# Three fused blocks on one core: an attention unit's order, the first loads, which rows of the third block stand in which stage, and a decay factor kept in three places

## The reference

```python
# first block: short conv, conformer conv (31 taps), differential attention
y_sc   = (sc_b * causal_dwconv(sc_c * sc_x, sc_conv)) @ sc_out
y      = causal_dwconv(a * sigmoid(gate), conf_conv) + conf_conv_b   # 31 taps
a      = softmax(q1 k1) - lam * softmax(q2 k2)                       # 4 heads x 4 query blocks
# third block: z, r are silu(...) rows, gates are sigmoid(...) rows, xs/bm/cm pass a 4-tap conv
o_a = rms_norm(gla(...), gla_norm_w) * silu(r)
o_b = ssd_scan forward + backward + d_skip * x;  o_b = rms_norm(o_b * silu(z))
merged = sigmoid(gate_a) * (o_a @ w_pa) + sigmoid(gate_b) * (o_b @ w_pb)
```

## Time and profile before

| | us |
|---|---|
| median of 3 runs (lowest, highest) | 3657.41 (3651.36, 3658.62) |
| the profiled execution | 3653.29 |
| its span | 3651.3 |

### The profile page before, as it was taken

The page is one execution under the profiler, slowest core; times in us unless marked ns, Lnnn a source line. Parts: engine busy times, 40 slices in busy tenths (PEclk is TensorE's granted clock), DMA queues, the critical chain, the costliest instruction groups (busy, mean ns, idle before and its releaser), DMA issues. The chain is left out here.

```text
span 3651.3 us, 44458 instructions
## 1 busy us (share of the span) xinstructions
PE 3279.2 (90%) x17672; PEld 2613.6 (72%) x17672; DVE 2141.3 (59%) x2499; ACT 1254.9 (34%) x1906; POOL 1360.4 (37%) x625
## 2 busy tenths in 40 slices
PE   7989998999989898988999988989989757789997
PEld 5767876888856677966888867767876545668885
DVE  6366965889855476344746574867974676531112
ACT  4223343323243332233323342333433354332222
POOL 3423434444422234434444432326631222334442
PEclk9989999999989999999999989989999879899998
DMA  3213354465333245344344232423334445422322
GB/s 115 87 58 113 118 159 152 144 224 180 127 113 99 75 133 157 123 163 155 121 145 155 69 111 89 153 83 118 105 111 126 156 141 162 133 81 81 110 84 66
DMA packets 237261, 447.05 MB, mean 122 GB/s; under 512 B 59792, under 2 KB 119888, under 8 KB 230272
## 3 DMA queue, kind: packets, MB, share of 16 engines
q1 hardware_dynamic: 229984, 433.73, 36.5%
q10 hardware_dynamic: 7072, 10.49, 0.8%
HBM read 394.78 MB, written 49.37 MB: 122 GB/s over the span
## 5 line engine op out<-in xcount | busy, mean ns | idle before, releaser
L356 POOL TENSOR_TENSOR third_feed_lo<-third_feed_raw,third_feed_hi 128x1024 fp32r<-128x1024 f32 (+3 forms) x191 | 445.4, 2335 | 836.2 <-ACT third_feed_hi L349 819.8
L356 POOL TENSOR_TENSOR second_feed_lo<-second_feed_raw,second_feed_hi 128x1024 fp32r<-128x1024 f32 (+3 forms) x182 | 405.4, 2229 | 667.0 <-ACT second_feed_hi L349 637.8
L356 POOL TENSOR_TENSOR first_feed_lo<-first_feed_raw,first_feed_hi 128x1024 fp32r<-128x1024 f32 (+4 forms) x182 | 394.9, 2174 | 601.0 <-ACT first_feed_hi L349 591.2
L273 PE MATMUL shared_ps<-third_h_hi,third_feed_hi 128*128 128x512 f32 (+1 forms) x776 | 327.4, 422 | 66.9 <-ACT lgate_rows_bend L875 14.5
L274 PE MATMUL shared_ps<-third_h_lo,third_feed_hi 128*128 128x512 f32 (+1 forms) x776 | 314.2, 405 | 0.0
L275 PE MATMUL shared_ps<-third_h_hi,third_feed_lo 128*128 128x512 f32 (+1 forms) x776 | 313.9, 405 | 0.0
L349 ACT ACTIVATE third_feed_hi<-third_feed_raw 128x1024 fp32r<-128x1024 f32 (+3 forms) x191 | 190.8, 1001 | 278.7 <-PE ffn_low L275 79.1
L349 ACT ACTIVATE second_feed_hi<-second_feed_raw 128x1024 fp32r<-128x1024 f32 (+3 forms) x182 | 173.9, 956 | 211.0 <-PE ffn_low L275 70.8
L273 PEld LDWEIGHTS shared_ps<-third_h_hi,third_feed_hi 128*128 128x128 f32 (+1 forms) x776 | 153.2, 197 | 116.2 <-issue 77.7
L273 PE MATMUL mixer_acc<-first_h_hi,first_feed_hi 128*128 128x512 f32 x544 | 224.4, 413 | 11.3 <-DVE first_h_lo L428 7.4
L349 ACT ACTIVATE first_feed_hi<-first_feed_raw 128x1024 fp32r<-128x1024 f32 (+4 forms) x182 | 168.5, 929 | 191.0 <-PE mixer_acc L275 64.2
(11 more groups left out here) (761 smaller groups left out, 8005.7 us busy)
## 6 DMA issues: line engine op xcount, KB each, us to landing
third_feed_raw<-in_stream SPq DMA_DIRECT2D x156, 512.0 KB, 3.4
second_feed_raw<-in_stream SPq DMA_DIRECT2D x130, 512.0 KB, 3.5
first_feed_raw<-in_stream SPq DMA_DIRECT2D x120, 512.0 KB, 3.3
ffn_ada_w<-in_w_ada SPq DMA_DIRECT2D x48, 1024.0 KB, 5.2
shared_seg<-scratch_cum SPq DMA_DIRECT2D x32, 512.0 KB, 6.1
scratch_gates<-mixer_gate ACTq DMA_DIRECT2D x32, 256.0 KB, 2.1
mix_gin<-scratch_gates SPq DMA_DIRECT2D x32, 256.0 KB, 3.1
shared_spare<-scratch_ecum SPq DMA_DIRECT2D x64, 128.0 KB, 4.3
```

The costliest lines, as they stand in the source:

```text
L273: nc.tensor.matmul(out, w_hi, x_hi, start=start, stop=False)
L356: eng.tensor_tensor(self.lo[:, p % self.cut, :n], self.raw[:, p % self.deep, :n], self.hi[:, p % self.cut, :n].bitcast(F32), ALU.subtract) ...
```

## The change

- SP issues the eight loads of x ahead of the first three weight pieces, and ACT squares x ahead of cutting the first two pieces.
- In units 0 to 3, `top(n+1)` and `take_taps(4)` stand in front of the wait for the row and its product. In units 4 and 5 the four taps stand in front of the second product (behind its `short_conv`) instead of behind it.
- The rows of the third block are dealt anew, the same number for each stage: context has 16 z and 4 r rows, gates 2 r and 8 gate rows, levels 24 conv and 2 r rows, gla 8 gate rows. The weight stream is put in the same order.
- e is held one direction at a time, in three places that are used in turn, each with a semaphore; part n (n = 2c+d) may be loaded once part n-3 has been read. SP loads parts 0 to 2 of group 0 in the gla stage (six DMAs in place of four), and the loads of parts 3 to 7 are put between the others. `tmp` moves into an existing tile to make room.
- In ssm, SP issues the loads of the x tiles 2 and 3 ahead of `load_gate` for tiles 2 and 3.

```diff
-            feed.load(sp, 3)
             for k in range(DT):
                 sp.dma_start(core.x[:, k], ...).then_inc(x_loaded[k], 16)
+            feed.load(sp, 3)
...
+            norm.scalar_squares(act)
             feed.split_hi(act, 2)
-            norm.scalar_squares(act)
             feed.split_hi(act, feed.cut)
...
                 mix(n)
                 if n < 4:
+                    top(n + 1)
+                    take_taps(4)
                     feed.done(dve, "sc", 2 * n + 1)
                     dve.wait_ge(act_free, 12 + n + 1)
                     v.tensor_tensor(prod[:, n], acc[:, 1], side[:, n % 2], ALU.mult).then_inc(dve_free, 1)
...
                     for j in (2 * n - 8, 2 * n - 7):
                         short_conv(j)
+                        if j % 2:
+                            take_taps(4)
                         feed.done(dve, "sc", 8 + j)
...
-                elif n + 1 < 16:
-                    top(n + 1)
-                take_taps(4)
+                elif n >= 6:
+                    if n + 1 < 16:
+                        top(n + 1)
+                    take_taps(4)
...
-                ssm.load_e(sp, 0, 0)
+                for n in range(3):
+                    ssm.load_e(sp, 0, n)
...
-    def load_e(self, sp, g, c):
+    def load_e(self, sp, g, n):
         by = self.dram["ecum"].rearrange("(d g j k) t -> d g k j t", d=2, g=4, j=4)
-        for d in range(2):
-            for k in range(2):
-                sp.dma_start(self.e[half(k), d], spread(by[d, g, k, :, c * P:(c + 1) * P], 64)).then_inc(self.e_in, 16)
+        c, d, place = n // 2, n % 2, (8 * g + n) % 3
+        for k in range(2):
+            sp.dma_start(self.e[place][half(k)], spread(by[d, g, k, :, c * P:(c + 1) * P], 64)
+                         ).then_inc(self.e_in[place], 16)
...
-                def load_e(g, c):
-                    if 4 * g + c:
-                        sp.wait_ge(read, 8 * g + 2 * c)
-                    loads.load_e(sp, g, c)
+                def load_e(g, n):
+                    sp.wait_ge(read, 8 * g + n - 2)
+                    loads.load_e(sp, g, n)
...
+                    load_x(g, 2)
+                    load_x(g, 3)
                     if g:
                         for j in range(2, 4):
                             load_gate(g - 1, j)
-                    load_x(g, 2)
-                    load_x(g, 3)
...
                     load_cum(g, 4)
+                    load_e(g, 3)
                     load_cum(g, 5)
-                    load_e(g, 1)
+                    load_e(g, 4)
                     load_cum(g, 6)
+                    load_e(g, 5)
                     load_cum(g, 7)
...
-                    load_e(g, 2)
+                    load_e(g, 6)
+                    load_e(g, 7)
                     dense.sync_gates(sp, pieces_by(g, 1, 1))
                     for j in range(2):
                         load_gate(g, j)
                     for n in range(2 if g < 3 else 0):
                         load_cum(g + 1, n)
-                    load_e(g, 3)
                     for n in range(2, 4 if g < 3 else 0):
                         load_cum(g + 1, n)
                     if g < 3:
                         load_start(g + 1)
-                        load_e(g + 1, 0)
+                        for n in range(3):
+                            load_e(g + 1, n)
...
-                    v.tensor_tensor(part, by_channel(ps[:, 2 + 2 * (c % 2)]), e[:, 0], ALU.mult).then_inc(read, 1)
+                    v.tensor_tensor(part, by_channel(ps[:, 2 + 2 * (c % 2)]), e[m % 3], ALU.mult).then_inc(read, 1)
+                    m += 1
+                    dve.wait_ge(e_in[m % 3], 32 * (m // 3 + 1))
...
-                stage_third_context(nc, core, feed, h, ps, z_rows + gate_rows[:4], half, b, attn)
-                stage_third_gates(nc, core, feed, h, ps, r_rows + gate_rows[4:6], half, b, by_tok)
-                stage_third_levels(nc, core, feed, h, ps, conv_rows + gate_rows[6:8], half, qk, b, attn)
+                stage_third_context(nc, core, feed, h, ps, z_rows + r_rows[:4], half, b, attn)
+                stage_third_gates(nc, core, feed, h, ps, r_rows[4:6] + gate_rows[:8], half, b, by_tok)
+                stage_third_levels(nc, core, feed, h, ps, conv_rows + r_rows[6:], half, qk, b, attn)
```

More of the change, by code:

```diff
@@ L1588, in _ @@
                         short_conv(j)
+                        if j % 2:
+                            take_taps(4)
                         feed.done(dve, "sc", 8 + j)
                         v.tensor_tensor(prod[:, j], work[:, j % 2], acc[:, j % 2], ALU.mult).then_inc(dve_free, 1)
-                        if j % 2 == 0 and n + 1 < 16:
+                        if j % 2 == 0:
                             top(n + 1)
-                elif n + 1 < 16:
-                    top(n + 1)
-                take_taps(4)
+                elif n >= 6:
+                    if n + 1 < 16:
+                        top(n + 1)
+                    take_taps(4)
             take_taps(200)
@@ L3707, in __init__ @@
         self.dram, self.b, self.c, self.x, self.seg, self.states, self.e = dram, b, c, x, seg, states, e
-        self.bc_in, self.s_in, self.e_in = (s.sem(n) for n in ("bc_in", "s_in", "e_in"))
+        self.bc_in, self.s_in = (s.sem(n) for n in ("bc_in", "s_in"))
+        self.e_in = [s.sem(f"e_in{n}") for n in range(3)]
         self.x_in = [s.sem(f"x_in{n}") for n in range(2)]
@@ L4263, in out @@
                         dve.wait_ge(added, 4 * g + c)
-                    v.tensor_tensor(by_channel(tmp[:]), by_channel(ps[:, 3 + 2 * (c % 2)]), e[:, 1], ALU.mult
+                    v.tensor_tensor(by_channel(tmp[:]), by_channel(ps[:, 3 + 2 * (c % 2)]), e[m % 3], ALU.mult
                                     ).then_inc(read, 1)
@@ L4365, in third_block @@
                 stage_third_begin(nc, core, feed, h, ps, (qk, attn, b), (scale1, shift1), v_tok)
-                stage_third_context(nc, core, feed, h, ps, z_rows + gate_rows[:4], half, b, attn)
-                stage_third_gates(nc, core, feed, h, ps, r_rows + gate_rows[4:6], half, b, by_tok)
-                stage_third_levels(nc, core, feed, h, ps, conv_rows + gate_rows[6:8], half, qk, b, attn)
+                stage_third_context(nc, core, feed, h, ps, z_rows + r_rows[:4], half, b, attn)
+                stage_third_gates(nc, core, feed, h, ps, r_rows[4:6] + gate_rows[:8], half, b, by_tok)
+                stage_third_levels(nc, core, feed, h, ps, conv_rows + r_rows[6:], half, qk, b, attn)
             s = core.scope(nc, inner, "ahead")
-            x, b_first = s.sb("x", [P, 2, T]), s.sb("b", [P, T])
+            x, b_first, e_last = s.sb("x", [P, 2, T]), s.sb("b", [P, T]), s.sb("e", [P, T])
             c_, e = (spare[:, 1024 * n:1024 * (n + 1)] for n in range(2))
-            loads = SsmLoads(dram, s, b_first, c_.rearrange("p (n t) -> p n t", n=2), x, seg, states,
-                             e.rearrange("p (d j t) -> p d j t", d=2, j=4))
+            e = [a.rearrange("p (j t) -> p j t", j=4) for a in (e[:, :T], e[:, T:], e_last[:])]
+            loads = SsmLoads(dram, s, b_first, c_.rearrange("p (n t) -> p n t", n=2), x, seg, states, e)
             stage_third_gla(nc, core, feed, h, ps, gate_rows[8:], (v_tok, b, attn), merged, loads)
@@ L4486, in stream @@
     by_row("z3", w, range(3104, 5152, P))
-    by_row("g3", w, range(8288, 8800, P))
-    by_row("r3", w, range(2048, 3072, P))
-    by_row("g3", w, range(8800, 9056, P))
+    by_row("r3", w, range(2048, 2816, P))
+    by_row("g3", w, range(8288, 9312, P))
     by_row("xbc3", w, range(5152, 8224, P))
-    by_row("g3", w, range(9056, 10336, P))
+    by_row("r3", w, range(2816, 3072, P))
+    by_row("g3", w, range(9312, 10336, P))
     by_row("pa3", i["w_pa_3"][0], columns)
```

5 lines of the change are left out of this document (3 added, 2 removed).

## The result

| | kernel before | changed kernel |
|---|---|---|
| median of 4 runs on one chip, us (lowest, highest) | 3655.32 (3651.36, 3658.62) | 3608.99 (3604.97, 3615.71) |
| ratio, 95% interval | | 0.988 (0.9862 to 0.9899) |
| profiled execution, us (its span) | 3653.29 (3651.3) | 3612.13 (3610.3) |
| PE busy, us | 3279.2 | 3267.8 |

The account below looks back on a forecast made before the run. PE, busy 90% of the span, was held by waits for DVE, late loads and a low clock; -28.5 - 2.5 + 2.4 - 5.8 + 1.5 - 25 = -57.9 from 3657.41 gave 3599 us, range 3588 to 3610 (62%), 3580 to 3621 with rivals.

Parts of the forecast that it names:

- Part 1: First block's units: maxima and taps ahead of the row remove 19.5 us of PE waits, clock gives 9; -28.5.
- the mix stays late: Rival, 8%: POOL's lock holds the mix twice a unit, waits only halved, -14 for -28.5; 3613 us.
- Part 2: Start of the first block: x loaded first, ACT's root at 23.0 against 25.91; -2.5, bounds 0 and -4.8.
- Part 3: Third block's rows dealt anew: context and levels +1.2 each, gates -5.8 (bounds -10 and 0).
- Part 4: Decay factor e in three places: gla +1.5 for six DMAs, ssm net -25 (bounds -8 and -38).
- It is wrong if [...] ssm is less than 12 us shorter: Sign of failure; the other was line 1230 in the first block keeping 10 us or more of PE waits.
- I charge 1.5 a group, some 4: ssm: cost of e's loads holding back later decay matrices in SP's list, the second 5.5 us later in groups 1 and 3.
- 6 of the 9.37: ssm, seam of groups 1 and 2: share of PE's wait for x gained by asking for x tiles 2 and 3 sooner.
- the seam of groups 0 and 1, at 7: ssm: PE's waits of 3.79 and 3.28 there were to go, -7.
- I take 4: ssm: 4 us for a granted clock that rises a little once the waits are gone.
- the cum loads take over: Rival, 18%: in ssm each group waits for its decay matrices instead of e; ssm gives -8, 3616 us.
- slower rival, SP's head-of-list waits: Rival, 2%: e's loads wait for reads and delay loads behind them in ssm, 66 us against 58 won; 3665 us.

Follow-up runs that it names:

- -31.1 alone: Kernel before with only the new order of the first block's units (maxima and taps ahead of the row's product): 3625.64 us, 0.9922.
- combined kernel: Changed kernel with ssm's matrices 5 and 7 sooner, factors 0 to 2 later, the root ahead of piece 3's cut, context's old rows: 3583.9 us, 0.9819.
- order only: Kernel before, e in its two places, only the load of a group's last e put sooner in SP's list: 3654.44 us, 1.0016.
- matrices first: Changed kernel with decay matrices 5 and 7 of a group asked for ahead of decay factors 3 and 5 in ssm: 3594.24 us, 0.9853.
- rows alone: Kernel before with only the third block's rows dealt anew: 3649.75 us, 0.9985.

## Why the prediction was right, and where it was not

The forecast's number held better than its sum. The change was to win 57.9 us and won 46 by the medians, 41 between the two profiled executions. That 3609.0 still lies in the likeliest case's own range, 3588 to 3610, has luck in it: the median of the kernel before came out 2.1 us lower (3655.32) than the 3657.41 that the forecast was taken from, and the first block gave 3 us more than its terms.

**Part 1, -28.5 against -31.1 alone.** Right in mechanism and nearly in size. The waits of units 1 to 4 went and the clock is at its higher level. The 1.57 and the 2 us in units 4 and 5 that were to stay didn't: PE waits at line 1230 nowhere. These, and a clock at 1.00 where 9 of 9.9 had been taken, more than cover the difference. The rule of the Trainium skill on the shared port (SBUF — State Buffer, "SBUF: two separate sides") agrees with what this trace shows of the mix, 2.70 us beside a cut and 0.49 without, as far as the blocking goes. But the held instruction reads one tile, not two: it isn't the case with two SBUF inputs that the prediction quoted, and that it falls under the section's other case, a 2-port perf mode, no run here shows. One hold a unit was in the estimate, and one came, so the rival "the mix stays late" falls.

**Part 2, -2.5 against -2.0 at unit 0.** Right, with the cap that was given for it: the root at 23.66 for a forecast of 23.0, behind the cut of piece 3. The combined kernel shows that this cut was the cap.

**Part 3, -3.4 against -0.1 in this pair of executions, -1.9 over all.** Gates -5.7 for -5.8, though by another way: the restart came 2.6 earlier, not 2 by a wait shortened to 6 or 7; PE waited longer, from an earlier point. Levels +1.2 as forecast. Context was mis-sized: +1.2 for the shaping behind the last row, and "two to four more shapings lie under PE's rows", at nothing. It is +4.4 here and +2.4 over all. The 1.2 at the end came as forecast, and what lies under PE's rows did cost nothing that shows in its waits. In this pair its waits for ACT's second eviction rose from 5.2 to 7.8 us, but over all executions they are 6.8 and 7.0. The term that was missing is 1.3 us of PE's own time at a lower granted clock, 0.967 and 0.952, whose cause stays open.

**Part 4, gla +1.5 against +1.2; ssm -25 against -12.8 over three executions (-8.3 in this pair).** This is the step that failed, as a size, and by the prediction's own sign: "It is wrong if [...] ssm is less than 12 us shorter" is met in this pair, and missed by 0.8 in the means. The waits for e went (8.0 us left, under the 15 forecast), the seam of groups 2 and 3 lost its 8.49, and the end came sooner. Four terms were too large or too cheap. First, "I charge 1.5 a group, some 4" for SP's order. The delay itself was sized rightly, 5.5 us forecast and 6.0 measured; its cost wasn't. ACT's wait for matrices rose by 13.0 and PE's for masks by 10.6, one of them in group 3 to 8.13 where 4.07 had been the longest. Taking that order away gave 5 us in ssm against the mean and 9.9 by the ratios' difference (0.27% of 3655), which is uncertain by 9. Second, "6 of the 9.37" at the seam of groups 1 and 2: I counted what x had been moved past, four gate loads of 2.2 us in all, and not what was put in ahead of it, six issues of e where four had stood, behind a list that was already late. Before, x went out 4.1 us after its place was free (2970.0 to 2974.13); in the changed kernel it is 6.9 (2936.3 to 2943.15), and it lands 5.3 us later in both. That is the 2.8 by which the wait of 9.37 grew. With e put behind x the waits for x fell by 5.5. Third, the seam of groups 0 and 1, at 7: its waits of 3.79 and 3.28 became 1.60 and 4.45, and PE comes to its wait of 4.75 in group 1 116.9 us after the stage's start, for 121.0. That is 4.1. Fourth, "I take 4" for the clock: the stage's granted clock went from 0.86 to 0.87 and PE's busy time from 285.1 to 283.2 us, 1.9.

Followed through the stage, PE is 4.1 us ahead there, 1.9 behind at its wait of 5.10 for xw past the seam of groups 1 and 2 (179.9 for 178.0), 7.9 ahead in group 3 (279.4 for 287.3), and 8 ahead at the end, where the tail's gain and the masks of group 3 cancel.

So ssm went some two thirds of the way (12.2 of 17 us, by the means) to the rival "the cum loads take over", whose -8 is what this one pair shows. The number held all the same since ssm is one term of six: -33.9, +4.4, -5.7, +1.2, +1.2 and -8.3 make -41.1.

The slower rival, SP's head-of-list waits, was given 2% at a price of 66 us. The mechanism is real: the kernel with order only is slower by 0.16% with PE's waits for x up by 15.6, and between the matrices it took 5 to 10 us of part 4's gain. Its price, 66 us, was far too high.

## What to carry to other kernels

When one engine issues all loads from one list, an edit there has to be read twice: what each load waits for (and so holds behind it), and how many issues now stand ahead of the load that the critical engine waits for. Price a load's new place by the read it waits for, taken from the consumer's timeline, and put loads whose wait is long over (e for the next group) behind the ones that are due at once (x, gates). And work that is ready belongs ahead of a wait, not behind it: two thirds of this kernel's gain (0.78 of 1.2%) come from the maxima and taps of the first units moved in front of one wait of an engine that works in order.

## What the runs showed that had not been expected

With SP's denser list the median time from issue to landing of a 512 KB decay matrix in ssm rose from 6.1 to 7.4 us, of a 256 KB x tile from 4.0 to 5.1, of a 128 KB load of e from 4.3 to 5.0 or 5.4. With the matrices first it was 6.6 for a matrix. What the loads share no run shows. In the seam of groups 1 and 2 SP issued 20 DMAs from 2926.09 to 2944.23; most of the issues took 0.43 to 0.62 us, four of them 1.45 to 3.82. And stages of identical code differ from one execution to the next in steps: 156.7 to 156.9 or 159.0 to 159.2 us for one stage of the second block, 618.2 to 619.0 or 621.2 to 621.6 for the first of the third, in kernels that differ in neither. The granted clock goes with these steps: in the first of the two stages it is 0.979 in the four short executions, with 143.6 to 143.8 us of PE's busy time, and 0.961 in nine of the ten long ones, with 146.0 to 146.1; "rows alone", the tenth, has 0.972 and 143.6. What sets the clock from one execution to the next stays open.
